# Slots of rounded weights and operands of tokens at other byte offsets in SBUF

## What is computed

```
layer 0:  proj = x @ w_in            (1024 x 4112), causal conv, gated delta rule, @ w_out (1024 x 1024)
          x = LN(alpha*x + h);  h = (silu(x @ w_gate) * (x @ w_up)) @ w_down      (d_ff 2816)
layer 1:  shared K/V = x @ w_kv;  q = x @ w_q;  banded softmax attention with sinks;  @ w_o
          x = LN(alpha*x + h)
          top-2 of 8 experts, each (silu(h[:, :2816]) * h[:, 2816:]) @ w_down[e],  h = x @ w_gu[e]
          x = LN(alpha*x + h)
```

## Time and profile before

| | us |
|---|---|
| median of 3 runs | 1298.13 |
| lowest, highest | 1297.95, 1301.44 |
| the profiled execution | 1302.06 |
| its span, first to last instruction | 1300.3 |
| TensorE (PE) busy | 1259.6 (97%) |
| VectorE (DVE) busy | 1003.1 (77%) |
| ScalarE (ACT) busy | 835.2 (64%) |

### The profile page before, as it was taken

The page is one execution under the profiler, slowest core; times in us unless marked ns, Lnnn a source line. Parts: engine busy times, 40 slices in busy tenths (PEclk is TensorE's granted clock), DMA queues, the critical chain, the costliest instruction groups (busy, mean ns, idle before and its releaser), DMA issues.

```text
span 1300.3 us, 16894 instructions
## 1 busy us (share of the span) xinstructions
PE 1259.6 (97%) x6781; PEld 1079.1 (83%) x6781; DVE 1003.1 (77%) x849; ACT 835.2 (64%) x842; POOL 98.5 (8%) x116
## 2 busy tenths in 40 slices
PE   8999999999999998999999999999999999999994
PEld 8997987888888987888888888888888888888883
DVE  6876844666645584788888888888898988898896
ACT  5794343545534464477777777777777777778772
POOL 4043210100001100300000000000000000001100
PEclk9999998999999999899999999999999999999997
DMA  9733011997554423599999999999999999999991
GB/s 316 260 144 130 1 34 65 386 371 248 193 194 152 172 67 124 191 383 406 390 385 401 384 389 373 386 388 374 388 386 372 390 390 371 383 383 367 388 395 39
DMA packets 188852, 375.76 MB, mean 289 GB/s; under 512 B 12240, under 2 KB 69696, under 8 KB 188768
## 3 DMA queue, kind: packets, MB, share of 16 engines
q1 hardware_dynamic: 179744, 345.02, 73.0%
q0 software_dynamic: 6864, 25.81, 5.2%
q10 hardware_dynamic: 2160, 3.79, 0.8%
HBM read 354.12 MB, written 20.45 MB: 288 GB/s over the span
## 4 chain that ended last, share of the span: by engine, by line
PE 87%; DVE 4%; ACT 3%; DMA 3%; issue 1%; SPq 1%; POOL 1%; DVEq 0%; ACTq 0%
PE ps L1419 84%; DMA raw<-in_ffn_w_gu 2%; PE ps L1827 1%; DVE lo L914 1%; DVE conv L995 1%; ACT hi L549 1%; DMA raw<-in_dn_w_in 1%; SPq L296 1%; PE ps L1820 0%; DVE x L1385 0%; ACT ps L564 0%; ACT pT L555 0%; ACT ps L602 0%; ACT zn L602 0%; DVE x L950 0%
## 5 line engine op out<-in xcount | busy, mean ns | idle before, releaser
L914 DVE TENSOR_TENSOR lo<-raw,hi 128x2048 fp32r<-128x2048 f32 x326 | 744.5, 2296 | 183.0 <-ACT hi L549 182.0
L549 ACT ACTIVATE hi<-raw 128x2048 fp32r<-128x2048 f32 x326 | 625.4, 1919 | 298.6 <-PE ps L1419 265.9
L1419 PE MATMUL ps<-hi,xg_hi 128*128 128x512 f32 x704 | 277.5, 394 | 0.1
L1419 PE MATMUL ps<-hi,xg_lo 128*128 128x512 f32 x704 | 274.5, 390 | 0.0
L1419 PE MATMUL ps<-lo,xg_hi 128*128 128x512 f32 x704 | 274.1, 389 | 0.0
L1419 PE MATMUL ps<-xT_both,hi 128*128 128x256 f32 (+1 forms) x896 | 224.1, 330 | 2.3 <-DVE xT_both L922 2.1
L1419 PE MATMUL ps<-xT_both,lo 128*128 128x256 f32 x624 | 175.8, 282 | 0.0
L1419 PEld LDWEIGHTS ps<-xT_both,hi 128*128 128x128 f32 x896 | 151.0, 190 | 19.7 <-issue 2.6
L1419 PEld LDWEIGHTS ps<-hi,xg_lo 128*128 128x128 f32 x704 | 132.1, 188 | 28.0
L1419 PEld LDWEIGHTS ps<-hi,xg_hi 128*128 128x128 f32 x704 | 132.2, 188 | 27.8 <-issue 0.8
L1419 PEld LDWEIGHTS ps<-lo,xg_hi 128*128 128x128 f32 x704 | 132.3, 188 | 26.6
(11 more groups left out here) (287 smaller groups left out, 1218.3 us busy)
## 6 DMA issues: line engine op xcount, KB each, us to landing
raw<-in_moe_w_gu SPq DMA_DIRECT2D x352, 512.0 KB, 7.2
raw<-in_moe_w_down SPq DMA_DIRECT2D x176, 512.0 KB, 6.6
raw<-in_ffn_w_gu SPq DMA_DIRECT2D x44, 512.0 KB, 8.2
raw<-in_dn_w_in SPq DMA_DIRECT2D x32, 512.0 KB, 8.9
raw<-in_ffn_w_down SPq DMA_DIRECT2D x22, 512.0 KB, 4.0
xe<-xTf POOLq DMA_DIRECT2D x1, 8192.0 KB, 29.1
raw<-in_dn_w_out SPq DMA_DIRECT2D x8, 512.0 KB, 3.9
ys<-xTf POOLq DMA_DIRECT2D x1, 4096.0 KB, 40.1
```

Source lines behind the costliest of these rows:

```text
L549: act.activation(slot(hi, j), slot(raw, j), ACT.Copy).then_inc(hi_ready, 1)
L914: dve.tensor_tensor(slot(lo, j), slot(raw, j), slot(hi, j).bitcast(F32), ALU.subtract).then_inc(lo_ready, 1)
L1419: return pe.matmul(dst, lhsT, rhs, start=start, stop=stop)
```

## The change

`hi` and `lo` become flat tensors with a few spare elements. Slot 0, 1, 2 of `hi` begins 0, 16, 40 elements further than before (0, 64, 160 bytes), slot 0, 1, 2 of `lo` 0, 8, 32 elements further (0, 32, 128 bytes) than its new base. Small unused tensors (`..._apart`, 8 to 32 elements) stand ahead of token operands. `raw` stays where it was. Everything behind `hi` moves: `lo` starts 192 bytes further, `xT_both` and `hT_hi` 352, `hT_lo` 384, `oT_hi` 416, `oT_lo` 512, `xg_hi` 384, `xg_lo` 448, `hE_hi` 576, `hE_lo` 640; `x` and all small tensors shift by 352 to 640 too. All shifts are multiples of 32 bytes. Then `hi` slot 2, `lo` slot 1, `xT_both`, `hT_hi` and `oT_hi` begin 32 bytes past a multiple of 64, and the distances between a matmul's two operands differ from pair to pair. No instruction is added, removed or moved, no wait changes, and each instruction reads and writes as many elements as before.

```diff
+HI_AT = (0, 16, 40)
+LO_AT = (0, 8, 32)
...
-        hi = sb("hi", [P, CUT, UNIT], F32R)
-        lo = sb("lo", [P, CUT, UNIT], F32R)
+        hi = sb("hi", [P, CUT * UNIT + HI_AT[-1] + 8], F32R)
+        lo = sb("lo", [P, CUT * UNIT + LO_AT[-1] + 8], F32R)
...
             hT_hi = sb("hT_hi", [P, 2 * FC, T], F32R, where=a)
+            sb("hT_lo_apart", [P, 8], where=a)
             hT_lo = sb("hT_lo", [P, 2 * FC, T], F32R, where=a)
...
+            sb("oT_hi_apart", [P, 16], where=a)
             oT_hi = sb("oT_hi", [P, KD, T], F32R, where=a)
+            sb("oT_lo_apart", [P, 24], where=a)
             oT_lo = sb("oT_lo", [P, KD, T], F32R, where=a)
...
         xg = sb("xg", [P, D])
+        sb("xg_hi_apart", [P, 8])
         xg_hi = sb("xg_hi", [P, KD, P], F32R)
+        sb("xg_lo_apart", [P, 16])
         xg_lo = sb("xg_lo", [P, KD, P], F32R)
         sgE = sb("sgE", [P, 2, 512])
         actE = sb("actE", [P, 2, 512])
+        sb("hE_hi_apart", [P, 32])
         hE_hi = sb("hE_hi", [P, 2 * FC, P], F32R)
+        sb("hE_lo_apart", [P, 16])
         hE_lo = sb("hE_lo", [P, 2 * FC, P], F32R)
...
         def slot(buf, j):
-            return buf[:, j % (RAW if buf is raw else CUT), :]
+            if buf is raw:
+                return buf[:, j % RAW, :]
+            at = j % CUT * UNIT + (HI_AT if buf is hi else LO_AT)[j % CUT]
+            return buf[:, at:at + UNIT]
```

More of the change, by code:

```diff
@@ L577, in _ @@
             act.sem_inc(raw_in[0], 16)
-            act.activation(hi[:, 0, 0:UNIT // 2], raw[:, 0, 0:UNIT // 2], ACT.Copy).then_inc(first_hi, 1)
+            act.activation(slot(hi, 0)[:, 0:UNIT // 2], raw[:, 0, 0:UNIT // 2], ACT.Copy).then_inc(first_hi, 1)
             act.wait_ge(raw_in[0], 32)
-            act.activation(hi[:, 0, UNIT // 2:UNIT], raw[:, 0, UNIT // 2:UNIT], ACT.Copy).then_inc(hi_ready, 1)
+            act.activation(slot(hi, 0)[:, UNIT // 2:UNIT], raw[:, 0, UNIT // 2:UNIT], ACT.Copy).then_inc(hi_ready, 1)
             cut_hi(1)
@@ L977, in _ @@
             dve.wait_ge(first_hi, 1)
-            dve.tensor_tensor(lo[:, 0, half[0]], raw[:, 0, half[0]], hi[:, 0, half[0]].bitcast(F32), ALU.subtract).then_inc(first_lo, 1)
+            dve.tensor_tensor(slot(lo, 0)[:, half[0]], raw[:, 0, half[0]], slot(hi, 0)[:, half[0]].bitcast(F32), ALU.subtract).then_inc(first_lo, 1)
             dve.wait_ge(hi_ready, 1)
-            dve.tensor_tensor(lo[:, 0, half[1]], raw[:, 0, half[1]], hi[:, 0, half[1]].bitcast(F32), ALU.subtract).then_inc(lo_ready, 1)
+            dve.tensor_tensor(slot(lo, 0)[:, half[1]], raw[:, 0, half[1]], slot(hi, 0)[:, half[1]].bitcast(F32), ALU.subtract).then_inc(lo_ready, 1)
             cut_lo(1)
```

## The result

The changed kernel is slower: 1313.95 us in the median of 4 runs (1312.72 to 1317.89) against 1298.04 us (1296.38 to 1301.44), a ratio of 1.0125 with a 95% interval of 1.0107 to 1.0143, 15.9 us. That is outside the predicted range of 1287 to 1309. The profiled execution has a span of 1312.4 us, 12.1 more than before.

A forecast was written before the change was run, and what follows sets the result against it. The prediction took TensorE's own rate in the experts to bound the kernel. Its terms for TensorE, VectorE and ScalarE, and DMAs were each 0, summing to 0 us and so 1298 us, range 1287 to 1309.

The forecast's parts named there:

- What bounds the kernel: Whole kernel: TensorE busy 1259.6 of 1300.3 us; in the experts only a change in its own rate moves the end.
- The value I take is 0: TensorE term, 5288 float32r matmuls: their fixed part does not depend on the distance between operands, 0 us.
- Rows 7: Product with `wab`, 16 weight columns, eight distances: 117.2 ns each, leaving 2.8 ns for distance and narrower weights together.
- Rows 9: Plain float32 matmuls: 111.4 ns with weights `g` at 4-byte steps, 111.3 with `Nm` and `Dm`; read as no difference.
- 0.74 to no effect: Whole kernel: chance given to nothing moving, a time within 0.3% of before.
- At best 65 us less: TensorE's lower bound: fixed part falls to about 2 ns, saving 45.0 us, 9.7 us and 10.4 us.
- the 11.2 ns: Best-case saving for each of 864 matmuls of 256 columns, 9.7 us in all.
- the 29.5: Best-case saving in ns for each of 352 pairs in the dense mixer, 10.4 us in all.
- At worst 40 us more: TensorE's upper bound: another 14.2 ns on 2808 matmuls whose stream starts 32 bytes past a multiple of 64.
- The faster rival: TensorE: part of the fixed part was a collision between weights' read and stream's; 1283 us, lower end 1233, chance 0.13.
- The slower rival: TensorE: streams starting 32 bytes past a multiple of 64 cost 6.3 ns, 2808 matmuls, 17.7 us; 1316 us, chance 0.13.
- VectorE, ScalarE, DMAs: Other engines and transfers: cost 0, VectorE and ScalarE hidden behind TensorE; VectorE's cut to stay at median 2292 ns.

The follow-up runs named there:

- e8: Kernel before plus groups of 16 512-column matmuls after the experts, with 32 to 128 weight columns and further distances; with 32 columns a group takes 3.78 us.
- e10: Kernel before plus 64 groups of 256-column matmuls at distances in 4-byte steps, then four of plain float32; 113.3 ns at distance 320, 120 at 256.
- e3: Kernel before with everything from raw on moved 32 bytes further, all distances kept; 1298.39 us, ratio 0.9989.
- e9: Kernel before plus 64 groups of 16 512-column matmuls, distances 256 to 508 in 4-byte steps; steps settle between 226.7 and 236.7 ns.
- e12: Kernel before with x and xT_both 192 bytes further, other token operands kept at 0 modulo 256; 1297.78 us, ratio 0.9993.
- e4: Kernel before, slots kept, token operands further by: xT_both 32 bytes, hT 64, oT 96, xg 128, hE 192; 1310.31 us, one execution.
- e6: Kernel before, slots kept, token operands moved to distances xT_both 160, hT 192, oT 224, xg 480, hE 0; 1315.03 us, one execution.
- e1: Kernel before, slots kept, with x, all token operands and small tensors at the changed kernel's addresses; 1315.91 us, ratio 1.011.
- e7: Kernel before plus groups of 16 matmuls after the experts, distances 0 to 480 in 32-byte steps, 512 then 256 columns; 3.75 to 3.83 us with 512.
- e14: Kernel before plus groups of 16 matmuls, 128 to 512 streamed columns at distances 0, 64, 96, 192; distances differ by 2.4 ns at 256 columns, 7 at 512.
- e13: Kernel before plus groups of 24 512-column matmuls, weights, stream or both moved 96 bytes in turn; distance 0 alone settles at 226.7 ns, 96 alone at 234.3.

## Why the prediction was wrong

**What bounds the kernel: right.** TensorE's rate in the experts carried nearly the whole result, some 15.7 of 15.9 us, and the prediction named it as the only place where a byte offset could act.

**The step that failed** is "The value I take is 0" for TensorE, which should have been 3168 x 5.0 ns, and about 5 ns for the 552 other wide ones: 18 us, less some 1 to 2 for narrower ones. In its place the runs showed a term that depends on the layout, 226.7 to 236.7 ns for the same matmul. The value rested on two witnesses, and neither was of the kind in question. Rows 7 had 16 weight columns; e8 shows that with 32 or 64 columns the distance makes no difference (3.78 us each), with 128 it does. Their stream had 256 columns besides, where distance 256 is not a cheap place but a dear one (e10), so that 117.2 against 120.0 was no upper bound for anything. Nor was it steady: e3 has a mean of 114.4 ns there with every distance as before, where the trace of before has 117.7. Rows 9 were plain float32, which e10 shows to be indifferent. The trace of before could not decide, since all pairs of the kind that matters had one distance; the prediction said so in its last sentence and still gave 0.74 to no effect. A witness of another shape or type should have widened the chances, not narrowed them.

**The bounds.** At best 65 us less: of the 45 us for 512 columns nothing was to be had, no distance goes below 226.7 ns (e9). With 256 columns e12 had 4.3 of the 11.2 ns, and a pair in e4 and e6 6.6 of the 29.5. At worst 40 us more held as a number only, since the mechanism that it priced, the start of the stream, costs nothing (e3).

**The faster rival** assumed that the common distance is a bad one. For 512 columns it was among the best. That the two reads disturb each other depending on their distance is right; the sign was the other.

**The slower rival** gave 1316, near the 1314 measured, by a wrong mechanism, which is luck. e3 moves every stream 32 bytes past a multiple of 64 at a ratio of 0.9989, and in e1 the experts' streams did not move at all.

**VectorE, ScalarE, DMAs: right.** The cut is at 2270, 2292 and 3827 ns (least, median, most) after, against the earlier trace rows. The conv projections got shorter by 0.5 us in the piece of 326, which the prediction had at 0.

The Trainium skill ("TensorE: Matmul & The Clock Gate", "Step-by-step: what each phase is for") lets the weights' load take nothing from the running stream. For float32r with 512 columns the runs show otherwise: the same matmul takes 6 to 7 ns more than 226.7 when only the distance to the weights' address is another (e7). Its fixed 2.5 ns ("Wait — 56ns, not 53.3ns?") do not hold for float32r, where no distance brought less than 13.3 ns at 512 columns. They would fit plain float32 here, 215.8 ns for a record of 256 columns, if a record passes its columns twice (213.3 ns); no run shows that it does.

## What to carry to other kernels

Where float32r matmuls of 512 columns bound a kernel, keep every stream a multiple of 256 bytes from the weights of the next matmul, slots used in turn and both parts of a split operand included, and check it after each small tensor that is put ahead of them: 32 bytes cost 2.6% of each such matmul (227.2 to 233.2 ns). For other widths this place isn't the best one (e10, e14) and has to be measured. A very regular step in a trace can mean that nothing depends on the layout, or that everything has the same layout. Only a witness of the same shape and type tells the two apart, and where there is none a measurement of 16 matmuls at each of a few distances at the kernel's end settles it in one run.

## What the runs showed of the hardware that was not expected

- The steps of equal matmuls lock into cycles of one to some ten matmuls. Their means are often 226.7, 230.0 or 233.3 ns with 512 columns (544, 552, 560 cycles of 2.4 GHz), but not always, and a distance that differs by 4 bytes can lock elsewhere (256: 226.7, 260: about 232 ns).
- float32r carries 13.3 ns beyond 213.3 at the best distance for 512 columns (e9), and a load of only 32 columns makes it no shorter: a group of 16 takes 3.78 us against 3.74 to 3.76 (e8).
- One displaced load among four costs almost as much as four (233.3 against 234.3 ns, e13).
- Why the level is what it is at a given distance, and what inside TensorE makes the two reads meet, stays open; the runs give the table, not the circuit. Open too is why single slots in the changed kernel differ from the table, and why e3's pairs are 2.7 ns shorter than before at the same distances.
